# One layer of a streaming encoder: 112 candidate sums, eight more plain U tiles, an early last norm and sixteen kept GELUs

## The reference, cut to what matters

```
q = (h @ wq) as 8 heads x 2 halves x 128;  s = q . subkeys      # 128 keys a half
sv, si = top_k(s, 16)                                           # for each half
comb = sv[:, :, 0, :, None] + sv[:, :, 1, None, :]              # 16 x 16 = 256 sums
cs, ci = top_k(comb, 16); ia, ib = si0[ci // 16], si1[ci % 16]
idx = ia * 128 + ib; g = softmax(cs)
a = u_tab[idx] . h; w = g * gelu(a); peer = sum of w * v_tab[idx]
h = LN(alpha * h + peer + sigmoid(h W_g + b_g) * (p W_p))
```

## Time and profile before

| | |
|---|---|
| median of three runs | 1415.41 us (1413.83 to 1418.49) |
| the profiled execution: own time, span | 1415.96 us, 1414.1 us |
| TensorE busy | 1337.5 us (95%) |
| VectorE busy | 1179.9 us (83%) |
| ScalarE, GpSimd busy | 660.7 us, 557.7 us |
| mean granted clock of TensorE | 0.98 |
| moved by DMA | 381.33 MB, 270 GB/s in the mean |

### The profile page before, as it was taken

How to read it: one execution, slowest core, us unless ns; L and a number is a source line. 1 busy time by engine, 2 the same in 40 slices (tenths; PEclk the granted TensorE clock), 3 DMA queues, 4 the chain that set the end, 5 groups by cost and what they waited for, 6 DMA issues and landing times.

```text
span 1414.1 us, 23312 instructions
## 1 busy us (share of the span) xinstructions
PE 1337.5 (95%) x7689; PEld 722.9 (51%) x7689; DVE 1179.9 (83%) x2324; ACT 660.7 (47%) x910; POOL 557.7 (39%) x352
## 2 busy tenths in 40 slices
PE   5989999999997999999989999999998999999994
PEld 3544445545654666666645555555553444444441
DVE  6652749999997999999778878788889888988888
ACT  4542455536667666766533333334333333433332
POOL 2640233344555432333234544445656342322221
PEclk9999999999998999999989999999999999999997
DMA  7222032234664999999899999999999999999981
GB/s 296 76 89 75 30 127 86 86 119 135 186 185 128 326 365 353 350 376 367 322 295 340 325 333 330 320 319 376 363 362 339 377 391 391 384 392 381 366 267 60
DMA packets 147211, 381.33 MB, mean 270 GB/s; under 512 B 11601, under 2 KB 70225, under 8 KB 144977
## 3 DMA queue, kind: packets, MB, share of 16 engines
q1 hardware_dynamic: 110288, 246.39, 49.7%
q0 software_dynamic: 36864, 134.23, 25.8%
HBM read 339.16 MB, written 41.42 MB: 269 GB/s over the span
## 4 chain that ended last, share of the span: by engine, by line
PE 68%; DVE 21%; DMA 5%; issue 4%; ACT 2%; SPq 0%; POOL 0%; DVEq 0%; ACTq 0%; POOLq 0%
PE bank L594 33%; PE bank L583 9%; PE bank L585 9%; PE bank L584 9%; DVE area L1382 2%; DVE area L1374 2%; DVE area L1376 2%; DVE area L1371 2%; DVE area L1412 2%; DVE area L1379 2%; PE bank L611 1%; PE bank L787 1%; DVE area L1386 1%; PE bank L789 1%; DMA ple_sb<-v_rows_dram,expert_id 1%
## 5 line engine op out<-in xcount | busy, mean ns | idle before, releaser
L594 PE MATMUL bank<-cut,area 128*128 128x512 f16 x2328 | 513.1, 380 | 15.2 <-DVE area L1564 10.0
L583 PE MATMUL bank<-hT,cut 128*128 128x384 f16 (+1 forms) x1232 | 413.9, 336 | 12.5 <-ACT gelu_out L1051 7.9
L584 PE MATMUL bank<-hT,cut 128*128 128x384 f16 (+1 forms) x1232 | 413.8, 336 | 0.0
L585 PE MATMUL bank<-hT,cut 128*128 128x384 f16 (+1 forms) x1232 | 413.8, 336 | 0.0
L594 PEld LDWEIGHTS bank<-cut,area 128*128 128x128 f16 x2328 | 227.9, 98 | 289.2 <-issue 8.9
L1168 DVE SCALAR_TENSOR_TENSOR cut<-raw,cut 128x1024 f16<-128x1024 f32 x242 | 298.7, 1235 | 73.5 <-ACT cut L846 71.9
L846 ACT ACTIVATE cut<-raw 128x1024 f16<-128x1024 f32 x242 | 250.6, 1054 | 196.7 <-PE bank L594 115.8
L532 POOL DMA_INDIRECT ple_sb<-u_rows_dram,expert_id x128 | 198.5, 1550 | 291.2 <-DVE dots_now L1485 281.2
L532 POOL DMA_INDIRECT ple_sb<-v_rows_dram,expert_id x128 | 172.1, 1344 | 254.7 <-DVE ple_gate L1576 240.7
L522 POOL TENSOR_TENSOR cut<-raw,cut 128x1024 f16<-128x1024 f32 x56 | 126.7, 2264 | 168.0 <-ACT cut L856 168.0
L1051 ACT ACTIVATE gelu_out<-bank 128x384 f32<-128x384 f32 x120 | 58.9, 491 | 257.5 <-PE bank L585 257.5
(11 more groups left out here) (140 smaller groups left out, 1134.5 us busy)
## 6 DMA issues: line engine op xcount, KB each, us to landing
raw<-tiles_dram SPq DMA_DIRECT2D x298, 512.0 KB, 6.0
gates_scratch<-area SPq DMA_DIRECT2D x12, 2048.0 KB, 11.0
area<-gates_scratch SPq DMA_DIRECT2D x32, 768.0 KB, 8.9
gelu_scratch<-gelu_out SPq DMA_DIRECT2D x72, 192.0 KB, 4.5
area<-gelu_scratch SPq DMA_DIRECT2D x18, 768.0 KB, 11.0
norm_rows<-norms_dram SPq DMA_DIRECT2D x3, 1024.0 KB, 8.1
hn<-x_dram SPq DMA_DIRECT2D x4, 512.0 KB, 5.6
ple_sb<-u_rows_dram,expert_id POOLq DMA_INDIRECT x128, 8.1
```

Of the source, the lines that this page charges most:

```text
L583: nc.tensor.matmul(dst, w[0], hT[:, 0, k, 0:width], start=(k == 0), stop=False)
L584: nc.tensor.matmul(dst, w[0], hT[:, 1, k, 0:width], start=False, stop=False)
L585: last = nc.tensor.matmul(dst, w[1], hT[:, 0, k, 0:width], start=False, stop=(k == KD - 1))
L594: mm = nc.tensor.matmul(bank[:, 2 * tt + h, :], lhs(a)[:, tt * P:(tt + 1) * P], cut[:, t.slot, b, h * HALF:(h + 1) * HALF], start=(first a ...
```

## The change

- The candidate sums are 112 instead of 256: the four best of the first half with all sixteen of the second (64), the other twelve with the four best of the second (48). `pick` turns an index of the 112 into the pair with a few short operations more.
- Eight U tiles more are computed before the pairs (U_PLAIN): 88 early tiles, 40 pairs in five eights, 88 late V tiles. They stand behind the gate rounds without gate work, one dot beside each. Three eights then take 24 dots each and two 24 sums, and the last eight V tiles take no sum.
- The GELUs of the eight plain tiles and of the last round stay on chip: sixteen instead of eight. 72 are stored, as before.
- SyncE stores a gate chunk two tiles later than it did, in the next half round or among the plain tiles.
- Exp goes from the first to the fourth softmax tile, the Sigmoid from the third to the sixth.
- The sparse token tile's last norm is made within the last eight V tiles: its sum, statistics and root behind the third, its scaling behind the fifth.

```
+U_PLAIN = 8
+U_KEPT = U_PLAIN + 8
-U_EARLY = U_TOPK + U_SOFTMAX + U_GATES
+U_EARLY = U_TOPK + U_SOFTMAX + U_GATES + U_PLAIN
-EIGHT_DOTS = (20, 20, 20, 20)
+KEPT_DOTS = 8
+EIGHT_DOTS = (24, 24, 24)
...
 SyncE, build_gates:
-                    sp.wait_ge(gates_out, 16 * it + 8 * s + 8)
-                    sp.dma_start(gates_dram[...], gate_chunk[:, s]).then_inc(gates_stored[s], 16)
+                        if j == 1 and s == 1:
+                            store_gates(2 * it, 0, 16 * it + 8)
+                        if j == 1 and s == 0 and not (isinstance(it, int) and it == 0):
+                            store_gates(2 * it - 1, 1, 16 * it)
...
+            for c in range(U_EARLY - U_PLAIN, U_EARLY):
+                load(Tile(T_U + c + LOAD_AHEAD))
+                if c == U_EARLY - U_PLAIN + 1:
+                    store_gates(GCH - 1, 1, TD // 4)
             load(Tile(T_BOTH + LOAD_AHEAD))
             for s in range(2):
                 sp.wait_ge(gates_stored[s], 16 * (GCH // 2))
             load_gates(0, U_EARLY, 0)
...
 TensorE, behind the rounds:
+            for c in range(U_EARLY - U_PLAIN, U_EARLY):
+                columns(Tile(T_U + c), u_index + c, c % 2, TD, 6)
...
 ScalarE:
-                if j == 0:
+                if j == 3:
                     act.wait_ge(gate_shift, 1)
                     nc.scalar.activation(picked[:, 2], picked[:, 2], ACT.Exp).then_inc(gate_exp, 1)
-                if j == 2:
+                if j == 5:
                     (Sigmoid of the four token tiles)
...
+            for j in range(U_PLAIN):
+                t = Tile(T_BOTH - U_PLAIN + j)
+                split_hi(t.plus(SPLIT_AHEAD))
+                gelu(t, j % 4, kept=U_KEPT - U_PLAIN + j)
...
+                    if end and v == 2:
+                        roots(2, 0)
...
 VectorE, add_sides and pick:
+                for t in range(TT):
+                    own.mark(nc.vector.tensor_tensor(
+                        sums[:, t, 0:WIDE * K]..., top_v[:, 0, t, 0:WIDE]..., top_v[:, 1, t, :]..., ALU.add))
                 own.mark(nc.vector.tensor_tensor(
-                    sums..., top_v[:, 0]..., top_v[:, 1]..., ALU.add))
+                    sums[:, :, WIDE * K:]..., top_v[:, 0, :, WIDE:]..., top_v[:, 1, :, 0:NARROW]..., ALU.add))
...
-                own.link(nc.vector.tensor_copy(half_h, half_i))
+                own.link(nc.vector.scalar_tensor_tensor(out=half_h[:, 0], ...))
+                own.link(nc.vector.tensor_scalar(start_f[:, 0], ...))
+                own.link(nc.vector.scalar_tensor_tensor(out=start_f[:, 1], ...))
+                own.link(nc.vector.tensor_tensor(half_h[:, 1], sum_i, start_f[:, 1], ALU.subtract))
...
+            for c in range(U_PLAIN):
+                split_lo(Tile(T_BOTH - U_PLAIN + c + SPLIT_AHEAD))
+                for j in range(KEPT_DOTS * c // U_PLAIN, KEPT_DOTS * (c + 1) // U_PLAIN):
+                    dot(j, (U_GATES + j) // ROW_RING)
+            keep_dots(U_GATES, KEPT_DOTS)
...
 VectorE, late:
+                if not end:
+                    weights_now(first + 8 * e, 8)
...
-                    if end:
-                        add_row(v, first + 8 * e + v, first // ROW_RING + 2 * e + v // ROW_RING)
+                    if end and v == 2:
+                        final_rows(0)
+                    if end and v == 4:
+                        layer_norm(2, 0)
```

More of the change, by code:

```diff
@@ L244, in layer @@
         replaced = part([2 * TT, NKEY])
-        sums = part([TT, K * K])
-        sums_rep = part([TT, K * K])
+        sums = part([TT, N_CAND])
+        sums_rep = part([TT, N_CAND])
         top_v = part([2, TT, K])
@@ L250, in layer @@
         sum_i = part([TT, K], U32)
[L251 removed]
+        quarter_i = part([2, TT, K], U32)
+        start_f = part([2, TT, K])
         half_h = part([2, TT, K], F16)
@@ L461, in late @@
                         load_gates(2 * EIGHTS + 2 * e + s + 2, VG * (2 * e + s + 2), s)
-            with sp.Fori(0, N_LATE // 8 - 2) as e:
+            with sp.Fori(0, N_LATE // 8 - 1 - U_KEPT // 8) as e:
                 late(e)
-            late(N_LATE // 8 - 2)
-            late(N_LATE // 8 - 1)
+            for e in range(N_LATE // 8 - 1 - U_KEPT // 8, N_LATE // 8):
+                late(e)
             for i, t in enumerate(FINAL_ORDER):
@@ L1143, in _, with late @@
                 both(e)
-            def late(e):
+            def late(e, end=False):
                 fixed = isinstance(e, int)
@@ L1630, in _ @@
                 own.turns, own.count = (count + 1) * (e - 1), before
-                both(e, lambda j: dot(j, U_GATES // ROW_RING + rounds * e + j // ROW_RING), count)
-                keep_dots(U_GATES + count * e, count)
+                both(e, lambda j: dot(j, first // ROW_RING + rounds * (e - 1) + j // ROW_RING), count)
+                keep_dots(first + count * (e - 1), count)
                 assert own.count - before == count + 1
@@ L1642, in _, with final_rows @@
                 first += count
-            def late(e):
-                fixed = isinstance(e, int)
-                end = fixed and e == N_LATE // 8 - 1
-                weights_now(first + 8 * e, 8)
-                for v in range(8):
-                    if not end:
-                        add_row(v, first + 8 * e + v, first // ROW_RING + 2 * e + v // ROW_RING)
-                    t = Tile(T_LATE + 8 * e + v) if fixed else Tile(T_LATE + v, 8, e)
-                    if not fixed or t.n + SPLIT_AHEAD + 1 < T_ALL:
-                        make_late(e, v + 3)
-                    if not fixed or t.n + SPLIT_AHEAD < T_ALL:
-                        weight_low(N_BOTH + 8 * e + v + 2, (v + 2) % RING)
-                        split_lo(t.plus(SPLIT_AHEAD))
-                    if end:
-                        add_row(v, first + 8 * e + v, first // ROW_RING + 2 * e + v // ROW_RING)
-            before = own.count
-            with dve.Fori(0, N_LATE // 8 - 2) as e:
-                own.turns, own.count = e, before
-                late(e)
-            own.turns, own.count = 0, before + N_LATE // 8 - 2
-            late(N_LATE // 8 - 2)
-            late(N_LATE // 8 - 1)
-            for i, t in enumerate(FINAL_ORDER):
+            def final_rows(i):
+                t = norm_order(2)[i]
                 if t == ND:
@@ L1684, in _, with late @@
                 row_moments(2, EPS / ALPHA ** 2, i)
-                if i:
+            def late(e):
+                fixed = isinstance(e, int)
+                end = fixed and e == N_LATE // 8 - 1
+                if not end:
+                    weights_now(first + 8 * e, 8)
+                for v in range(8):
+                    if not end:
+                        add_row(v, first + 8 * e + v, first // ROW_RING + 2 * e + v // ROW_RING)
+                    t = Tile(T_LATE + 8 * e + v) if fixed else Tile(T_LATE + v, 8, e)
+                    if not fixed or t.n + SPLIT_AHEAD + 1 < T_ALL:
+                        make_late(e, v + 3)
+                    if not fixed or t.n + SPLIT_AHEAD < T_ALL:
+                        weight_low(N_BOTH + 8 * e + v + 2, (v + 2) % RING)
+                        split_lo(t.plus(SPLIT_AHEAD))
+                    if end and v == 2:
+                        final_rows(0)
+                    if end and v == 4:
+                        layer_norm(2, 0)
+            before = own.count
+            turns = N_LATE // 8 - 1 - U_KEPT // 8
+            with dve.Fori(0, turns) as e:
+                own.turns, own.count = e, before
+                late(e)
+            own.turns, own.count = 0, before + turns
+            for e in range(turns, N_LATE // 8):
+                late(e)
+            for i in range(1, TT):
+                final_rows(i)
+                if i > 1:
                     layer_norm(2, i - 1)
```

60 lines of the change are left out of this document (38 added, 22 removed).

## The result

The changed kernel takes 1397.66 us in the median of four runs (1392.83 to 1400.32), the kernel before 1415.43 us beside it; the ratio is 0.9868, with a 95% interval of 0.9836 to 0.9900. Forecast were 1392.5 us, a ratio of 0.9838, and a range of 1387 to 1400: the median lies in that range, but above the forecast's own 1389.5 to 1396. The profiled execution took 1397.13 us, its span is 1395.3 us, 18.8 us shorter than that of before; the prediction had summed 22.9.

What follows compares the result with a forecast made beforehand. TensorE was taken to bound the kernel, busy 1337.5 of 1414.1 us. Gains of 8.7 (softmax), 9.3 (plain U tiles) and 4.9 (tail) summed to 22.9 us, giving a 1392.5 us median; range 1387 to 1400.

Steps and rivals of the forecast that it cites:

- Pace of PE, and long waits as the thing to look at: Whole kernel: PE's own work stays, 3.9 us per U or V tile; only PE's gaps and the slow clock behind them count.
- The 112 sums: VectorE's candidate search: 3.4 us less a head, 27 us for eight, as slack; Exp's operand ready at about 401 us.
- The softmax tiles: Softmax to gate rounds: the 7.2 us wait goes, a 2.1 us wait at the Sigmoid comes; 8.7 us gained, ends 6 and 11.2.
- I charge no slow stretch: Behind the new 2.1 us wait at the Sigmoid: no clock loss, since a 2.8 us wait elsewhere left the clock at 1.00.
- Table loads: ScalarE around Exp and Sigmoid: 1.28 us per table change, from the rows; at the skill's 2.66 us, time would be about 1397.5.
- The plain U tiles: Ahead of the first weighted V tile: the 10.0 us gap shrinks to a 0.7 us wait; 9.3 us gained, ends 8 and 10.
- no wait over 1 us: Sign of being right: PE has no such wait between the last gate product and the first weighted V tile.
- Dots and sums: Pairs of U and V tiles: three rows a pair cost nothing; the 2.2 and 2.8 us waits before the late tiles stay.
- Rival (3): First 24 pairs: gathered rows return late and PE waits each pair; at 1.5 us a pair, 1428.5 us; chance 0.03.
- The tail: Last V tiles to the end: early sparse norm gains 4.9 us net of a 1.8 us PE wait, ends 2 and 6.7.
- Rival (1): Softmax, plain tiles and tail: new waits short or absent, 27.9 us gained, time 1387.5 us; chance 0.10.
- rival (2): Sigmoid, picks or last eight tiles: new waits long, clock lost or ScalarE held; 16 us gained, 1399.5 us; chance 0.12.

Runs made afterwards that it cites:

- the repetition: The changed kernel timed and profiled again with nothing altered: 1393.17 us, ratio 0.9858 to the kernel before.
- The halved Sigmoid: Changed kernel with Exp ahead of the first softmax tile and the Sigmoid split, two token tiles ahead of the third and two ahead of the sixth: 1394.54 us.
- the late norm: Changed kernel with the sparse token tile's norm made behind the last V tile again, as before: 1397.70 us, ratio 0.9859 to the kernel before.
- the three edits: Changed kernel with Sigmoid in two halves, gate loads three tiles earlier, sparse norm behind the first of the last eight V tiles: 1388.76 us.

## Why the prediction was right, and where its terms were off

The direction, the places and the order of size were right; the total gain in the first profile is 18.8 us where the sum said 22.9. In the repetition it is 23.0, of which 2.4 are the stretch to G, where nothing was changed: that the repetition meets the sum is in part luck. The forecast's ratio of 0.9838 lies just outside the repetition's interval (0.9841 to 0.9874). The gain was put somewhat too high.

- **Pace of PE, and long waits as the thing to look at**: right. Nearly all of the gain is in the two waits of the earlier trace rows and in the tail.
- **The 112 sums**: VectorE was early, but with Exp's operand by some 15 us (413.7 against 428.5), not 27. The last head ended at 410.8 where "near 400" was said. The searches came out as worked out: on the sums they take 36.8 us where they took 60.7, 3.0 us a head less. The additions didn't. The four of 64 take 12.1 us over eight heads and the one of 192 takes 2.8, where one addition of 1024 took 17.3: 2.4 us less and not 8.8. And operations that the change left alone are some 4 us longer in sum; what lengthens them was not looked into. With 256 sums put back the last head ends at 433.5 us, 22.7 later. The text called the 27 us slack; the 256 sums cost 4.1 us up to R, 3.3 of them at the picks (a wait of 4.70 us where 1.36 is).
- **The softmax tiles**: 7.4 us came of 8.7. The wait was 2.31 us (2.1 said), the additions ended at 451.10 (451.1 said), R was at 453.78 (452.4 said). The step that failed is "I charge no slow stretch": behind this wait the clock was 0.50 for 3 us, 1.6 us of matmuls. A clock of 0.5 behind the Sigmoid was one of the prediction's own signs of being wrong, and it came. The halved Sigmoid confirms it, with 3.2 us for wait and clock together.
- **Table loads**: the rows again show the GELU begin 1.29 us after the load begins (443.83 to 445.12), and the wait of 2.31 us is the one that this duration gives. By the Trainium skill ("ScalarE: Activation LUTs", What ACT_TABLE_LOAD costs) a switch takes 2.66 us; the trace disagrees with the page here.
- **The plain U tiles**: 8.2 us came of 9.3: R to W is 5.9 us shorter and the slow clock behind the old gap, 2.3 us and in the old W to L, is gone. The loads of the gates came 9.7 us before W, as worked out (7.0 and 2.6). The wait ahead of W was 1.26 us where 0.7 was said, and "no wait over 1 us" so came out just wrong; the rest is one more wait of 0.7 us in the rounds, into which PE now goes earlier.
- **Dots and sums**: right that three rows a pair cost PE nothing: in the three eights with 24 dots VectorE waited for rows seven times, 10.3 us, and PE never. Rival (3) did not come. "Both stay", said of the waits at the turn, was off: 7.8 us in the first profile and 6.5 us lost in the repetition, where before had 5.7. That is 1 to 2 us, and no more than this stretch varies by; whether the change causes it is not shown.
- **The tail**: 5.4 us net came where 4.9 was said (6.8 in the tail less 1.45 from L to E; the wait in the run 1.27 us of 1.8). But the reason was half wrong. The prediction gave the whole gain to the early norm; 4.2 us come from the last eight tiles taking no sums, as the late norm's rows show, and the early norm nets 1.1.

Sum of the first profile: 7.4 + 8.2 - 2.1 + 5.4 = 18.9, against 18.8. Rival (1) did not come, since both new waits were there; rival (2) came in one of its parts, the clock behind the Sigmoid.

## What to carry to other kernels

Price a new wait of TensorE with the slow clock behind it, even if one as long elsewhere in the trace had none. When a stage is made shorter, look at what PE waits for in the next one: here one-hot rows and the loads of the gates gave 2.7 of 3.2 us back, and only with the loads issued earlier did the gain come through. So try two such edits together before giving up on one. And where an engine waits at a place in a written order, take work away from it before rearranging that work: six sums left out showed in one run that VectorE's time was not what was short, but the rows that it waited for.

## What the runs showed of the hardware

The clock's fall depends on more than the length of a wait. Behind 2.31 us of waiting at the Sigmoid the granted clock fell to 0.50 in the changed kernel, and G to R repeats within 0.1 us in every kernel with that wait. With 256 sums a wait of 2.38 us near the same place left it at 1.00 (448 to 452 us). At the turn it stayed at 1.00 behind waits of 2.66 and 2.82 us in the changed kernel, and fell behind one of 3.30 us in the repetition. The window from 1040 to 1045 us there, with 16 matmuls where 25 start at the full clock:

```profile
1040.00:1045.00 5.00, 5.00 (x16) 1.91 (x17) 5.00 (x7) 1.62 (x3) 3.00 (x2) 0.66 0.81 268
```

In the three edits it fell behind 2.37 us (clock 0.66 from 1030 to 1035, 17 matmuls). It was each time one of the two levels, 2.4 or 1.2 GHz; which waits bring it down was not settled. The Trainium skill ("TensorE: Matmul & The Clock Gate", Part 1: The HAM clock gate) names these same two states; that much the trace agrees with.
